# Thirty-two weight rests of a gate and an attention projection: from GpSimd to VectorE

## What is computed

```
gate = sigmoid(rmsnorm(h, norm_ple) @ ple_gate_w + ple_gate_b)
h = h + gate * (p @ ple_w)
x = rmsnorm(h, norm_final)                      # end of the first block
h2 = rms_norm(x, norm_g) * (1 + scale) + shift  # beginning of the second
q, qi, ckv, ki, wi = columns of h2 @ w_in       # what sparse attention needs
```

## Time and profile before

| | |
|---|---|
| median of three runs | 2457.36 us (2456.05 to 2461.05) |
| the profiled execution | 2459.38 us, its span 2457.4 us |
| PE busy | 2355.6 us, 96% of the span |
| DVE busy | 1675.8 us, 68% |
| ACT busy | 1013.8 us, 41% |
| POOL busy | 760.8 us, 31% |
| granted PE clock, mean | 0.989 of full speed |

### The profile page before, as it was taken

How to read it: one execution, slowest core, us unless ns; L and a number is a source line. 1 busy time by engine, 2 the same in 40 slices (tenths; PEclk the granted TensorE clock), 3 DMA queues, 4 the chain that set the end, 5 groups by cost and what they waited for, 6 DMA issues and landing times. The chain is left out here.

```text
span 2457.4 us, 42274 instructions
## 1 busy us (share of the span) xinstructions
PE 2355.6 (96%) x17029; PEld 1903.3 (77%) x17029; DVE 1675.8 (68%) x2676; ACT 1013.8 (41%) x1723; POOL 760.8 (31%) x404
## 2 busy tenths in 40 slices
PE   7998999999999999999999899999999998988998
PEld 6887878887888888887877568788786667876886
DVE  6112543189789787897675599999997765556842
ACT  4213563355344343455543464544434652214231
POOL 3221334421000000005573226547443203222774
PEclk9999999999999999999999999999999999999999
DMA  3112412245552735403235104234234002004323
GB/s 143 44 53 70 141 39 101 63 189 199 234 185 81 278 116 215 168 33 98 75 113 170 53 28 135 78 118 134 66 129 146 27 18 64 21 30 153 141 77 112
DMA packets 92466, 266.50 MB, mean 108 GB/s; under 512 B 9544, under 2 KB 22896, under 8 KB 85104
## 3 DMA queue, kind: packets, MB, share of 16 engines
q1 hardware_dynamic: 85360, 251.21, 29.8%
q10 hardware_dynamic: 6912, 12.59, 1.4%
HBM read 214.85 MB, written 49.95 MB: 108 GB/s over the span
## 5 line engine op out<-in xcount | busy, mean ns | idle before, releaser
L332 PE MATMUL ps<-region_rounded,weights_hi_by_slot 128*128 128x512 f32 x1280 | 509.6, 398 | 19.4 <-DVE region_rounded L654 13.9
L334 PE MATMUL ps<-region_rounded,weights_lo_in_place 128*128 128x512 f32 x1280 | 500.3, 391 | 0.0
L333 PE MATMUL ps<-region_rounded,weights_hi_by_slot 128*128 128x512 f32 x1280 | 499.8, 390 | 0.0
L326 POOL TENSOR_TENSOR weights_lo_in_place<-wbuf,weights_hi_by_slot 128x1024 fp32r<-128x1024 f32 x130 | 322.3, 2483 | 489.5 <-ACT weights_hi_by_slot L322 489.2
L332 PEld LDWEIGHTS ps<-region_rounded,weights_hi_by_slot 128*128 128x128 f32 x1280 | 241.5, 189 | 79.2 <-issue 25.9
L333 PEld LDWEIGHTS ps<-region_rounded,weights_hi_by_slot 128*128 128x128 f32 x1280 | 241.7, 189 | 52.2 <-issue 3.3
L334 PEld LDWEIGHTS ps<-region_rounded,weights_lo_in_place 128*128 128x128 f32 x1280 | 241.2, 188 | 50.9
L322 ACT CAST weights_hi_by_slot<-wbuf 128x1024 fp32r<-128x1024 f32 x130 | 134.9, 1044 | 153.8 <-DMA wbuf<-w_o 47.8
L1872 POOL TENSOR_TENSOR tmp<-tmp 128x512 f32<-128x512 f32 x14 | 21.3, 1525 | 540.7 <-ACT tmp L1682 540.3
L1450 PE MATMUL ps<-region_rounded,weights_hi_by_slot 128*128 128x512 f32 x448 | 175.4, 392 | 4.7 <-DVE region_rounded L1972 2.7
L1450 PE MATMUL ps<-region_rounded 128*128 128x512 f32 x448 | 175.2, 391 | 1.4 <-DVE region_rounded L1972 1.4
(11 more groups left out here) (425 smaller groups left out, 4872.5 us busy)
## 6 DMA issues: line engine op xcount, KB each, us to landing
region_rounded<-scratch_mlp_lo SPq DMA_DIRECT2D x21, 1024.0 KB, 4.9
region_rounded<-scratch_mlp_hi SPq DMA_DIRECT2D x21, 1024.0 KB, 6.9
wbuf<-w_hn SPq DMA_DIRECT2D x37, 512.0 KB, 4.1
wbuf<-w_mlp SPq DMA_DIRECT2D x32, 512.0 KB, 5.9
region<-w_mlp SPq DMA_DIRECT2D x32, 512.0 KB, 6.3
wbuf<-w_in SPq DMA_DIRECT2D x25, 512.0 KB, 3.7
region<-xT SPq DMA_DIRECT2D x24, 512.0 KB, 6.5
xtra<-w_ada SPq DMA_DIRECT2D x48, 256.0 KB, 3.1
```

Of the source, the lines that this page charges most:

```text
L326: self.nc.gpsimd.tensor_tensor(self.m.lo4[:, n % SLOTS, :], self.m.raw4[:, n % SLOTS, :], self.m.hi4[:, n % SLOTS, :].bitcast(F32), ALU.su ...
L332: nc.tensor.matmul(out, m.hi4[:, s, w], m.rounded(hi + k, half(hf)), start=(k == 0), stop=False)
L333: nc.tensor.matmul(out, m.hi4[:, s, w], m.rounded(lo + k, half(hf)), start=False, stop=False)
L334: return nc.tensor.matmul(out, m.lo4[:, s, w], m.rounded(hi + k, half(hf)), start=False, stop=(k == KT - 1))
```

## The change

POOL keeps the rests of P0+2 and P0+3. The rests of the gate units from P0+4 on and of the attention units are made by DVE, with the same instruction and the same semaphore: after `scale_gate(i)` in round i from 1 on, and after the copy of bank i in the attention loop. In round 1 DVE waits first until POOL has made the rests up to P0+3.

```diff
@@ POOL
                 if i == 0:
                     st.lo(pool, P0 + 2)
                     st.lo(pool, P0 + 3)
-                elif i == 1:
-                    st.lo(pool, P0 + 4)
-                else:
-                    st.lo(pool, P0 + i + 3)
                 if i >= 2:
                     add_gained(i - 2)
             add_gained(2 * KT - 2)
             add_gained(2 * KT - 1)
-            for i in range(2 * NA):
-                if A0 + i + 3 < st.units:
-                    st.lo(pool, A0 + i + 3)
@@ DVE
+            def unit_lo(n):
+                dve.wait_ge(st.hi_ready, n + 1)
+                nc.vector.tensor_tensor(m.lo4[:, n % SLOTS, :], m.raw4[:, n % SLOTS, :], m.hi4[:, n % SLOTS, :].bitcast(F32),
+                                        ALU.subtract).then_inc(st.lo_ready, 1)
+
             for i in range(2 * KT):
                 scale_gate(i)
+                if i == 1:
+                    dve.wait_ge(st.lo_ready, P0 + SLOTS)
+                if i:
+                    unit_lo(P0 + i + 3)
                 if i == KT + 3:
                     join_inverse(0)
...
                 nc.vector.tensor_copy(m.chunk(QA + ATT_ORDER[u], half(hf)), m.ps[:, j % 4, :]).then_inc(taken, 1)
+                if A0 + i + 3 < st.units:
+                    unit_lo(A0 + i + 3)
                 if i == 2:
                     join_variance(1)
```

## The result

| | before | after |
|---|---|---|
| median | 2458.89 us (20 runs, 2451.34 to 2462.64) | 2461.85 us (20 runs, 2458.13 to 2468.05) |
| ratio to before, 95% interval | | 1.0017 (1.0010 to 1.0024), or +4.2 us (2.5 to 5.9) |
| profiled execution, its span | 2459.38, 2457.4 us | 2460.38, 2458.6 us |
| granted PE clock, mean | 0.989 | 0.984 |

The change makes the kernel slower by 4.2 us. The forecast was +1.1 us, called no change; the rival in which the clock falls was priced at +4.7 us.

What follows compares the result with a forecast made beforehand. TensorE, busy 96% of the span, bounds the kernel, waiting 2.1 us on DVE's L2267. Rounds 12 to 15 add 0.31 + 3 x 0.27 = 1.1 us, all else 0: median 2458.5 us, range 2454.8 to 2462.6.

Steps and rivals of the forecast that it cites:

- the rival in which the clock falls: Attention unit 0: PE's longer wait drops its clock to half for 6 us; +4.7 us, median 2462.1, chance 0.12.
- The price of a rest: One moved 128x1024 subtraction on DVE takes 1.16 us, at the upper end 2.27 beside POOL work.
- Rounds 12 to 15: Last gate rounds, where DVE is slower than PE: 0.31 us for round 12, 0.27 for each other, 1.1 together.
- The sum on tile 7: The four late gate rounds' cost, 1.1 us, all falls on PE's wait in attention unit 0, 2.1 to 3.2 us.
- L2267 against POOL's sums: Late gate rounds: DVE's L2267 pair keeps its 2.80 us, since POOL's sums keep their place against it; no gain.
- The faster rival: Late gate rounds: L2267 pairs shorten from 2.80 to about 1.4 us, closing PE's wait; -2.1 us, median 2455.3, chance 0.12.
- Start of the gate: The first moved rest, P0+4, ends at 1164.3, before PE needs it at 1164.92; cost 0 us.
- The spare of 0.6: Slack at the gate's start between the end of rest P0+4 and PE's need of it, 0.6 us.
- The attention loop: Seventeen rests, 20 us, fit into DVE's 49.6 us idle there, so PE never waits; cost 0 us.
- What 0.2% tells apart: A measurement of the whole kernel tells about 0.2% (4.9 us) from no change; same 0.85, slower 0.10, faster 0.05.

Runs made afterwards that it cites:

- Experiment 7: Kernel after, with the attention input's two tiles made ahead of the gate's addition in rounds 12 to 15, on DVE and ACT; 2455.61 us against 2459.65, ratio 0.9981.
- experiment 2: Kernel after with only the attention rests on DVE, the gate rests back on POOL; 2458.06 us, ratio 0.9996 to the kernel before.
- Experiments 6 and 9: Kernel before plus a useless DVE reciprocal in round 15: 160 columns 2463.17 us, ratio 1.0009 (also 64 columns, profiled once); 9: two more profiles with 160, stretches 132.12, 132.91.
- experiment 1: Kernel after with only the gate rests on DVE, the attention rests back on POOL; 2464.0 us against 2459.07 before, ratio 1.0018.
- 11, after again: The kernel after, unedited, timed once more; 2464.59 us against 2460.22 before, ratio 1.0018.
- 4, after, work in the wait: Kernel after with the last six embedding matmuls put ahead of tile 7 of attention unit 0, into PE's wait; 2460.23 us, ratio 1.0008 to before.
- 3, late rests on POOL: Kernel after with the four rests of rounds 12 to 15 back on POOL, the other 28 on DVE; 2457.61 us, ratio 0.9988 to before.

## Why the prediction was right or wrong

- **The price of a rest: right.** Forecast 1.16 us, measured 1.13 of the queue in rounds 12 to 15. In rounds 4 to 7 a rest lasts 1.47 to 1.50, beside POOL's L1920, and once 2.11, at the start of the attention loop; nobody waits for it there. The Trainium skill, "SBUF — State Buffer", section "SBUF: two separate sides", says that a DVE operation with two SBUF inputs and a GpSimd one that reads SBUF exclude each other for a whole instruction; the trace agrees, with the addition's 1584 ns turned to 692.
- **Rounds 12 to 15: right.** Round 12 takes 7.81 us where before it took 7.52, +0.29 (forecast 0.31); rounds 13 and 14 take 7.79 where they took 7.56 and 7.54, and round 15 brings 0.22 up to its second L2267, so +0.22 to +0.25 each (0.27). The sum on tile 7 is 0.99 (1.1).
- **L2267 against POOL's sums: right.** 2.80 became 2.81 us. The faster rival needed it to shorten. Experiment 7 shows that it can, by another order on DVE and ACT.
- **Start of the gate: right.** L1925 started at 1152.21, at the end of ACT's cast, and the embedding's rest took 2.28 us where it took 5.34. The rest of P0+4 ended at 1160.9; product 4 starts at about 1161.5. The spare of 0.6 was 0.5.
- **The attention loop: right,** by experiment 2: 0 us.
- **The clock: wrong, and it decides.** The failed step is the rival's point and its chance: "It decides if the first piece comes nearer to 3.60 than to 2.69 us", with a chance of 0.12. The piece was 2.38 us, so by that sentence the clock had to stay. It fell in 5 of 6 executions. The step took two rows, one fall and one that was kept, for the two sides of a boundary in length. Experiments 6 and 9 show that there is none between them: the same 3.3 us gave both outcomes, and one kernel's 2.4 us too. With a fall in most executions the forecast had to be the rival's median, 2462.1 us, not 2458.5. Its price for half clock, 3.0 us for 6 us of it, was too high as well. The runs show 2.3 where it lasts 6.8 us, because half clock costs nothing while PE would wait anyway: tile 8 starts 1.69 us behind tile 7 with it and without. From tile 8's start to the end of the half clock it is 4.85 us (1259.22 to 1264.07), and half of that is 2.4. That the rival's +4.7 lies near the measured +4.2 is in part luck: in this stretch lateness and clock cost 2.8 us on the mean, and the rival had nothing outside it.
- **What 0.2% tells apart.** I gave +1.1 to +4.7 as hardly to be told from no change. With 20 runs a side the interval of the +4.2 us was 2.5 to 5.9, so the sign was plain below that bound.

**What stays open.** The stretch explains 2.8 us; the medians say +4.2, +4.4 and +4.9 (the change twice, and experiment 1), and their intervals reach down to 2.0. The second place fits the rest: in the six profiles of the changed kernel and experiment 1 the distance there is 25.5 us on the mean, and 23.1 in the seven of kernels whose wait in unit 0 is 1.4 us or less, 2.4 us more. The two together, 5.2 us, are a little over the medians. The granted clock of every execution, not only of the profiled ones, points the same way. A mean that is lower by 0.001 stands for some 4.9 us more at half clock (2 x 0.001 x 2459).

| kernel, executions | mean clock, and of before | half clock more than before |
|---|---|---|
| after, 20 (before: the 35 of experiment 1) | 0.9840, 0.9868 | 13 us |
| 1, gate only, 11 | 0.9836, 0.9868 | 15 us |
| 11, after again, 11 | 0.9826, 0.9859 | 16 us |
| 6, before + 160 columns, 10 | 0.9839, 0.9869 | 15 us |
| 4, after, work in the wait, 11 | 0.9862, 0.9868 | 3 us |
| 3, late rests on POOL, 11 | 0.9881, 0.9868 | -6 us |

The 95% intervals of the last column are 5 to 9 us to either side. The 35 executions of before in the first row were made with experiment 1, not with the 20. Unit 0's fall is 5 us of half clock on the mean of the six profiles, so most of the 13 to 16 us lies elsewhere, and none of it is seen once work fills the wait or the late rests are back on POOL. What the profiles don't show is a loss in the sum: from the end of the attention loop to the end of the span those six take 1069.9 to 1081.8 us, mean 1074.5, and the other eleven 1069.1 to 1081.2, mean 1074.8; further falls, which differ from execution to execution, spread these times by 12 us. What decides in one execution whether the clock falls wasn't settled either, nor how the late wait and the second place are linked.

## What to carry to other kernels

Where TensorE waits for a queue, price what is put ahead of the awaited work in that queue, even if it is 1.1 us and the engine has idle time elsewhere: here 4 of 32 moved instructions made the whole loss. Add the clock to the price of a wait as a chance, not as a threshold: a lateness of 1 us cost 2.8 on this stretch, and 4.2 to 4.9 in the whole. Then look whether the awaited work can come earlier in its queue, or other matmuls into the wait: the first gave 4.7 us below the kernel before, the second 3.6 us of stretch back in the changed one.

## What the runs showed of the hardware

- TensorE's clock fell after waits of 2.38 to 2.40 us in 5 of 6 executions and stayed after one of 3.28 us. The same program differs from execution to execution, so one profile says nothing sure about a wait of this length. With waits up to 1.39 us, or none, it didn't fall there in any of 7 profiles. In 2 of the executions with a fall it came only after PE had worked again for 2.0 and 1.7 us.
- A fall of 17.1 us some 780 us later stood in 6 of the 7 profiles with a fall in unit 0 and in none of the 10 without; the distance it lies in was 26.97 to 27.22 us with it and 22.02 to 24.32 without.
- Half clock can make waits look shorter in the idle column: 2.4 us after against 2.1 before, with PE 1.0 us late and then 2.3 more. Distances between the starts of the same matmuls show it; idle sums don't.
